# Layer 0's RMS norms taken one stream after the other, and a reordered prologue, in a two-layer fp32 backbone

## What is computed

```python
for l in range(DEPTH):                                   # DEPTH = 2
    sh1, sc1, g1, sh2, sc2, g2 = split(silu(c) @ w_mod[l] + b_mod[l])      # and mod_c from c_ctx
    h = modulate(rms_norm(x, ln1_g[l]), sh1, sc1)        # both streams
    proj = h @ w_in[l]
    att, y_conv, y_sc = attention(proj), conformer_conv(proj), short_conv(proj)
    x = x + g1 * merge_branches(gates, att, y_conv, y_sc, w_o[l])
    h2 = modulate(rms_norm(x, ln2_g[l]), sh2, sc2)
    x = x + g2 * swiglu(h2, w_ff1[l], w_ff3[l], w_ff2[l])                  # D_FF = 2816
return rms_norm(x, final_g)                              # latent stream alone
# modulate(x, shift, scale) = x * (1 + scale) + shift
# rms_norm(x, g) = x * rsqrt(mean(x * x) + eps) * g
```

## Time and profile before

| | |
|---|---|
| median of 3 runs | 1298.66 us (1297.06 to 1298.73) |
| profiled execution | 1295.26 us, span 1293.5 us |
| TensorE (PE) busy | 1230.8 us, 95% of the span |
| VectorE (DVE), ScalarE (ACT), GpSimd (POOL) busy | 876.1, 527.1, 53.5 us |
| mean granted TensorE clock | 0.984 of full speed |
| HBM read | 185.49 MB, 144 GB/s over the span |

### The profile page before, as it was taken

The page is one execution under the profiler, slowest core; times in us unless marked ns, Lnnn a source line. Parts: engine busy times, 40 slices in busy tenths (PEclk is TensorE's granted clock), DMA queues, the critical chain, the costliest instruction groups (busy, mean ns, idle before and its releaser), DMA issues.

```text
span 1293.5 us, 19441 instructions
## 1 busy us (share of the span) xinstructions
PE 1230.8 (95%) x7228; PEld 1030.4 (80%) x7228; DVE 876.1 (68%) x1344; ACT 527.1 (41%) x877; POOL 53.5 (4%) x52
## 2 busy tenths in 40 slices
PE   4999999999998979999999999799999998999997
PEld 3777776677886868888888888578789888999996
DVE  4555676768776377768765666778788766666565
ACT  4433445522423343222222223355664555644444
POOL 2000000000000300000000000300000002000002
PEclk9999999999999989999999999999999999999999
DMA  8838222124454516546565654435343574666662
GB/s 278 260 98 255 81 61 66 33 78 116 112 166 115 163 38 190 179 147 210 151 193 163 221 171 147 116 82 132 101 120 94 147 212 119 191 187 190 175 175 70
DMA packets 281601, 187.63 MB, mean 145 GB/s; under 512 B 12796, under 2 KB 270130, under 8 KB 281522
## 3 DMA queue, kind: packets, MB, share of 16 engines
q1 hardware_dynamic: 281521, 186.57, 49.5%
HBM read 185.49 MB, written 1.05 MB: 144 GB/s over the span
## 4 chain that ended last, share of the span: by engine, by line
PE 86%; DVE 6%; issue 4%; ACT 3%; DMA 1%; DVEq 0%; ACTq 0%; SPq 0%; POOL 0%; POOLq 0%
PE bank L1658 21%; PE bank L1660 21%; PE bank L1659 21%; PE scores L1910 2%; PE bank L1693 2%; PE bank L1694 2%; PE bank L1701 2%; PE bank L1893 2%; PE probsT L1919 2%; PE bank L1895 2%; PE bank L1894 2%; ACT Whi L345 2%; PE attended L1930 1%; DVE RSTD L1167 1%; DVE Wlo L356 1%
## 5 line engine op out<-in xcount | busy, mean ns | idle before, releaser
L1658 PE MATMUL bank<-Hhi,Whi 128*128 128x512 f32 (+2 forms) x1216 | 414.1, 341 | 4.7 <-DVE Wlo L356 4.7
L1659 PE MATMUL bank<-Hlo,Whi 128*128 128x512 f32 (+2 forms) x1216 | 409.7, 337 | 0.0
L1660 PE MATMUL bank<-Hhi,Wlo 128*128 128x512 f32 (+2 forms) x1216 | 409.7, 337 | 0.0
L356 DVE TENSOR_TENSOR Wlo<-Wraw,Whi 128x1024 fp32r<-128x1024 f32 (+4 forms) x328 | 320.7, 991 | 108.7 <-ACT Whi L345 107.0
L345 ACT ACTIVATE Whi<-Wraw 128x1024 fp32r<-128x1024 f32 (+4 forms) x330 | 277.7, 862 | 153.5 <-PE bank L1660 101.8
L1658 PEld LDWEIGHTS bank<-Hhi,Whi 128*128 128x128 f32 (+1 forms) x1216 | 229.9, 189 | 37.1 <-issue 7.7
L1659 PEld LDWEIGHTS bank<-Hlo,Whi 128*128 128x128 f32 (+1 forms) x1216 | 229.9, 189 | 25.7 <-issue 1.2
L1660 PEld LDWEIGHTS bank<-Hhi,Wlo 128*128 128x128 f32 (+1 forms) x1216 | 229.9, 189 | 25.3
L1658 PE MATMUL bank<-Uhi,Whi 128*128 128x512 f32 (+1 forms) x480 | 163.9, 341 | 0.6 <-DVE Ulo L1179 0.6
L1659 PE MATMUL bank<-Ulo,Whi 128*128 128x512 f32 (+1 forms) x480 | 162.3, 338 | 0.0
L1660 PE MATMUL bank<-Uhi,Wlo 128*128 128x512 f32 (+1 forms) x480 | 162.3, 338 | 0.0
(11 more groups left out here) (170 smaller groups left out, 1380.7 us busy)
## 6 DMA issues: line engine op xcount, KB each, us to landing
Wraw<-in_w_ff SPq DMA_DIRECT2D x120, 512.0 KB, 3.9
Wraw<-in_w_in SPq DMA_DIRECT2D x78, 512.0 KB, 4.0
ATT<-in_w_mod SPq DMA_DIRECT2D x58, 512.0 KB, 4.4
Wraw<-in_w_o SPq DMA_DIRECT2D x16, 512.0 KB, 3.8
ACC<-in_w_mod SPq DMA_DIRECT2D x14, 512.0 KB, 4.3
Wraw<-in_w_ff SPq DMA_DIRECT2D x16, 384.0 KB, 3.2
Wraw<-in_w_mla_o SPq DMA_DIRECT2D x8, 512.0 KB, 3.5
ATT<-in_w_mod SPq DMA_DIRECT2D x12, 256.0 KB, 5.4
```

What stands on the lines that cost most here:

```text
L356: last = eng.tensor_tensor(lo, raw, hi.bitcast(F32), ALU.subtract)
L1658: pe.matmul(dst, sh, mh, start=j == 0, stop=False)
L1659: pe.matmul(dst, sh, ml, start=False, stop=False)
L1660: last = pe.matmul(dst, sl, mh, start=False, stop=j == k - 1)
```

## The change

Four things. First, the two inner norms of layer 0 whose input comes from a product (behind w_o, and behind the FF towards layer 1) are taken stream by stream: of the last two output tiles (WHOLE = 6 on) the latent halves are computed first, then the context halves, and residual, square, sum, root, reciprocal and the normed blocks follow for each stream apart; the first tiles on the normed operand are also computed by halves. Modulation transposes that stood in or behind these places stand ahead of them, with FF_FOLDS and FF_SUMS moved by up to two tiles. Second, in the prologue x is transposed, squared and summed before ctx, by half tiles; the ten small loads are issued by ScalarE; the narrow chunk is loaded behind part 0 of the modulation weights and split behind its norm; both reciprocals stand ahead of VectorE's splits. Third, TensorE issues eight matmuls of ones by ones at the start. Fourth, at the end VectorE multiplies by the gain alone as tiles come, TensorE transposes between the last tiles, sums squares into one column per token, and the reciprocal root is applied to the transposed output by ScalarE and VectorE.

```diff
@@ constants @@
-FF_FOLDS = [4, 5, 6, 8, 9, 10, 12, 13, 14, *range(16, 27), 28, 29, 30, 32, *range(33, 65)]
-FF_SUMS = [14, 24, 34, 42, 50, 58, 66]
+FF_FOLDS = [4, 5, 6, 8, 9, 10, 12, 13, 14, *range(16, 63)]
+FF_SUMS = [14, 24, 32, 40, 48, 56, 64]
+WHOLE = DT - 2
+WARMING = 8
@@ SyncE, prologue (the ten small loads at lines 425 to 436 go) @@
-for n in range(AHEAD + 1):
+             ctx_in[0].rearrange("(t p) d -> p t d", p=P)).then_inc(x_in[1], 16)
+for n in range(AHEAD):
     project(0, n)
 ...
-sp.wait_ge(sq_done, DT)
+sp.wait_ge(sq_done, 2 * DT)
 ...
+if part == 0:
+    project(0, AHEAD)
@@ GpSimd: the last two tiles' squares are added by halves @@
+def add_halves():
+    for s in range(2):
+        look()
+        slot = at.square.n % 2
+        pool.wait_ge(sq_summed, at.added.n)
+        pool.wait_ge(sq_done, at.square.n + 1)
+        pool.tensor_tensor(SUM[:, half[s]], SUM[:, half[s]], SQ[:, slot, half[s]],
+                           ALU.add).then_inc(sq_summed, 1)
+        at.square.n += 2
+        at.added.next()
@@ ScalarE, prologue (the ten small loads stand first) @@
-for k in range(DT):
+def first_root(s):
+    act.wait_ge(sq_summed, (s + 1) * DT)
+    act.activation(ROOT[:, half[s]], (PV, S[1])[s][:, half[s]], ACT.Sqrt, bias=EPS, scale=1.0 / D).then_inc(root_done, 1)
+for i in range(2 * DT):
+    s, k = divmod(i, DT)
     t = at.tile()
     act.wait_ge(drained[t.bank], t.drained)
-    square(X[:, k, :], T, k, DT)
-at.added.n = DT
+    if i >= 2:
+        act.wait_ge(sq_summed, i - 1)
+    act.activation(SQ[:, i % 2, half[s]], X[:, k, half[s]], ACT.Square).then_inc(sq_done, 1)
+    at.square.next()
+    if i == DT + 2:
+        first_root(0)
+at.added.n = 2 * DT
 at.tile()
 look()
+first_root(1)
 look()
-act.wait_ge(sq_summed, DT)
-act.activation(ROOT[:, :], PV[:, :], ACT.Sqrt, bias=EPS, scale=1.0 / D).then_inc(root_done, 1)
 look()
 mod_row(0)
-look("rope")
@@ ScalarE, the seam @@
+look()
+for m in range(WHOLE, DT):
+    half_square(at.tile(), m, 0)
+half_root(0)
+t = at.tile()
+look()
+half_square(t, WHOLE, 1)
+for k in range(DT):
+    half_h(k, 0)
+    if k == 1:
+        half_square(at.tile(), WHOLE + 1, 1)
+    if k == 5:
+        half_root(1)
+for k in range(DT):
+    half_h(k, 1)
+at.added.n += DT
@@ VectorE, the seam and the prologue @@
+def half_h(s, between):
+    after_all()
+    for k in range(DT):
+        settle()
+        dve.scalar_tensor_tensor(Z[:, k % 2, half[s]], X[:, k, half[s]], AV[:, k, s:s + 1],
+                                 RSTD[:, half[s]], mult, mult).then_inc(z_done, 1)
+        if k:
+            half_low(k - 1, s)
+        if k in between:
+            between[k]()
+    half_low(DT - 1, s)
+roots = stat_root(0, 4) if mod else stat_root(1, 0)
+at.square.n += DT + 2
+residual(WHOLE, 0)
+look()
+residual(WHOLE + 1, 0)
+gains(l, mod, gain, 2)
+half_root(0, roots - 1)
+residual(WHOLE, 1)
+half_h(0, {1: lambda: residual(WHOLE + 1, 1), 2: look})
+half_root(1, roots)
+half_h(1, {})
 ...
-for k in range(DT):
+def first_reciprocal(s):
+    dve.wait_ge(root_done, s + 1)
+    mark(dve.reciprocal(RSTD[:, half[s]], ROOT[:, half[s]]))
+for i in range(2 * DT):
+    s, k = divmod(i, DT)
     t = full()
-    dve.tensor_copy(X[:, k, :], banks[t.bank][:, :]).then_inc(drained[t.bank], 1)
+    dve.tensor_copy(X[:, k, half[s]], banks[t.bank][:, half[0]]).then_inc(drained[t.bank], 1)
     at.square.next()
 through(t)
+first_reciprocal(0)
 t = full()
 for b, n in enumerate((ROWS, ROWS, 2 * NMOD * DT)):
     last = dve.tensor_copy(PAR[:, b, 0:n], banks[t.bank][:, b * P:b * P + n])
 last.then_inc(drained[t.bank], 1)
 through(t)
+first_reciprocal(1)
 at.split_by_slot = True
-look()
-look()
-dve.wait_ge(root_done, 1)
-mark(dve.reciprocal(RSTD[:, :], ROOT[:, :]))
-look()
-look("rope")
+for _ in range(AHEAD):
+    look()
@@ VectorE, start of layer 1, layer 0's residuals, and the end @@
-else:
-    normed_h(l, 0, 2)
-    mod_add_vector(*FF_VECTORS[-1])
-    dve.wait_ge(mod_done, at.turn)
+        if part == 0:
+            look("rope")
 ...
-    if l == 0 and j == 0:
-        dve.wait_ge(mod_done, at.turn)
-    if l == 0 and j == DT - 1:
-        mod_add_vector(0, 4, 2)
+        if l == 0:
+            dve.wait_ge(mod_done, at.turn)
     residual(j, 2)
     if j:
         look_and_fold()
-at.square.n += DT
-gains(l, 3, LN2, NS[l])
-take_root(TQ, stat_root(l, 4))
-normed_h(l, 3, NS[l])
+    if l == 0 and j == WHOLE - 1:
+        mod_add_vector(0, 4, 2)
+if l == 0:
+    seam(residual_half(2), look_and_fold, l, 3, LN2)
+else:
+    at.square.n += DT
+    gains(l, 3, LN2, NS[l])
+    take_root(TQ, stat_root(l, 4))
+    normed_h(l, 3, NS[l])
 ...
-residual(j, 5)
+through(residual(j, 5))
+finished(j)
 ...
-for k in range(DT):
-    dve.scalar_tensor_tensor(G[:, k, 0:SEQ], X[:, k, 0:SEQ], PAR[:, 3, FING + k:FING + k + 1],
-                             RSTD[:, 0:SEQ], mult, mult).then_inc(fin_z, 1)
+dve.wait_ge(root_done, stat_root(DEPTH, 0))
+dve.reciprocal(RT[:, 2:4], RT[:, 0:2]).then_inc(fin_root, 1)
+dve.wait_ge(fin_root, 1)
+for h in range(2):
+    dve.wait_ge(fin_turned, h + 1)
+    dve.tensor_scalar(X[:, 2 * h + 1, :], BY_TOKEN[1][h][:, :], RT[:, 3:4], None,
+                      mult).then_inc(out_scaled, 1)
@@ TensorE, the seam @@
+def half_product(t, slot, k, ops, s, a, b, ready):
+    oh, ol = ops
+    for j in range(a, b):
+        pe.wait_ge(op_lo, ready + j + 1)
+        w, dst = slice(j * P, (j + 1) * P), banks[t.bank][:, half[s]]
+        pe.matmul(dst, Whi[:, slot, w], oh[:, j, half[s]], start=j == 0, stop=False)
+        pe.matmul(dst, Whi[:, slot, w], ol[:, j, half[s]], start=False, stop=False)
+        last = pe.matmul(dst, Wlo[:, slot, w], oh[:, j, half[s]], start=False, stop=j == k - 1)
+    return last
+def seam_tiles(k, ops, ready):
+    slots = [chunk() for _ in range(2)]
+    squares, added = at.square.n, at.added.n
+    def half_total(t, s):
+        pe.wait_ge(sq_summed, added + DT - 1 + s)
+        pe.matmul(banks[t.bank][:, half[s]], ONES[:, :], SUM[:, half[s]], start=True, stop=False)
+        pe.wait_ge(sq_done, squares + DT + 2 * s)
+        pe.matmul(banks[t.bank][:, half[s]], ONES[:, :], SQ[:, (squares + 1) % 2, half[s]],
+                  start=False, stop=True).then_inc(tile_done, 1)
+    for slot in slots:
+        half_product(new_tile(), slot, k, ops, 0, 0, k, ready).then_inc(tile_done, 1)
+    latent, t = new_tile(), new_tile()
+    half_product(t, slots[0], k, ops, 1, 0, k // 2, ready)
+    half_total(latent, 0)
+    half_product(t, slots[0], k, ops, 1, k // 2, k, ready).then_inc(tile_done, 1)
+    half_product(new_tile(), slots[1], k, ops, 1, 0, k, ready).then_inc(tile_done, 1)
+    context = new_tile()
+    at.square.n += DT + 2
+    at.added.n += DT
+    return lambda: half_total(context, 1)
@@ TensorE, the tiles behind the seam (the last matmul of each tile in together(1, ..) signals tile_done) @@
+def staggered_tiles(ready, context_total, third_whole):
+    slots = [chunk() for _ in range(2)]
+    tiles = [new_tile() for _ in range(2)]
+    def together(s, slots, tiles, between=None):
+        r = ready + s * DT
+        for j in range(DT + 1):
+            if j < DT:
+                pe.wait_ge(op_hi, r + j + 1)
+                for t, slot in zip(tiles, slots):
+                    w, dst = slice(j * P, (j + 1) * P), banks[t.bank][:, half[s]]
+                    pe.matmul(dst, Whi[:, slot, w], Hhi[:, j, half[s]], start=j == 0, stop=False)
+                    pe.matmul(dst, Wlo[:, slot, w], Hhi[:, j, half[s]], start=False, stop=False)
+            if j:
+                pe.wait_ge(op_lo, r + j)
+                for t, slot in zip(tiles, slots):
+                    w, dst = slice((j - 1) * P, j * P), banks[t.bank][:, half[s]]
+                    last = pe.matmul(dst, Whi[:, slot, w], Hlo[:, j - 1, half[s]], start=False, stop=j == DT)
+                    if s and j == DT:
+                        last.then_inc(tile_done, 1)
+            if j == 4 and between:
+                between()
+    together(0, slots, tiles, context_total)
+    slots.append(chunk())
+    tiles.append(new_tile())
+    if third_whole:
+        half_product(tiles[2], slots[2], DT, (Hhi, Hlo), 0, 0, DT, ready)
+        together(1, slots, tiles)
+    else:
+        half_product(tiles[2], slots[2], DT, (Hhi, Hlo), 0, 0, DT - 1, ready)
+        together(1, slots[:2], tiles[:2])
+        half_product(tiles[2], slots[2], DT, (Hhi, Hlo), 0, DT - 1, DT, ready).then_inc(tile_done, 1)
@@ TensorE, prologue, start of layer 1, w_o, end @@
+for _ in range(WARMING):
+    pe.matmul(S[1][:, 0:P], ONES[:, :], ONES[:, :], start=True, stop=True)
 ...
+for i in range(2 * DT):
+    s, k = divmod(i, DT)
+    if k == 0:
+        pe.wait_ge(x_in[s], 16)
     t = new_tile()
-    for j in range(4):
-        src = G[:, 2 * j + k // 4, (k % 4) * P:(k % 4 + 1) * P]
+    for j in range(2):
+        src = G[:, 4 * s + 2 * j + k // 4, (k % 4) * P:(k % 4 + 1) * P]
```

(41 more changed lines are left out.)

197 lines of the change are left out of this document (130 added, 67 removed).

## The result

The changed kernel takes 1282.74 us (median of four executions, 1278.65 to 1283.61), the kernel before beside it 1298.10. The ratio is 0.9877, 95% interval 0.9860 to 0.9893. The profiled execution is the fastest of the four: 1278.65 us against 1295.26 before, 16.6 less, where the medians differ by 15.4. The forecast was 1281.2, or 17.5 less.

A forecast was written before the change was run, and what follows sets the result against it. The kernel was taken as bound by TensorE's matmuls, with only idle and half-clock time to win. Gains 5.6 + 3.85 + 4.8 + 3.3 = 17.5 us gave a median of 1281.2 us (profiled 1277.8), range 1277 to 1289.

The forecast's parts named there:

- Seam 1: Norm behind layer 0's w_o: taken stream by stream, 39.1 us becomes 33.5; gain 5.6 us, ends 3.0 and 6.5.
- Seam 2: Norm between layer 0's FF and layer 1: 35.75 us becomes 31.9; gain 3.85 us, ends 1.0 and 5.0.
- Rival 1: Clock falls to half in the two layer 0 norms, costing 2 to 4 us each; time 1286; chance 0.2.
- the clock read 0.50 in a seam: Sign at the two layer 0 norms: granted clock expected at 1.00 through both; 0.50 in either would make the prediction wrong.
- Prologue: Start of the kernel: TensorE's first operand matmul at 27.2 instead of 32.00; gain 4.8 us, ends 2.5 and 6.5.
- the early modulation weights: Prologue: first modulation weights issued at 10.5 instead of 15.86, landing near 20.5 and so off the path.
- the dummies: Prologue: eight dummy matmuls could delay the silu by 2 us or save up to 1.9 in transposes; taken as zero net.
- Rival 2: Prologue stays, its first operand bound by modulation weights or dummy matmuls; time 1285.7; chance 0.12.
- Tail: End of the kernel: scaling by the root moves behind the transposes; 12.65 us becomes 9.3, gain 3.3, ends 2 and 4.5.
- Rival 3: Prologue: full DMA engines hold back ScalarE's ten issues, delaying TensorE; slower than before, 1300 us and up; chance 0.04.
- rival 4: The two layer 0 norms don't overlap because a wait in TensorE's order ends late; 9 us less, 1290; chance 0.08.
- Folds: FF of layer 0: folds ending at position 62 instead of 64 fit behind the weight queue; cost 0, up to 1 us.

The follow-up runs named there:

- b1: The changed kernel with the norm behind layer 0's w_o put back as before: 1285.48 us, ratio 0.9906, 3.4 us over the changed kernel.
- b2: The changed kernel with the norm between layer 0's FF and layer 1 as before, moved modulation sum kept: 1282.65 us, ratio 0.9890.
- d1: The changed kernel with the ten small vector loads issued by SyncE again, behind the first three weight chunks: 1281.51 us, ratio 0.9877.
- a1: The changed kernel without the eight dummy matmuls at the start of TensorE's stream: 1280.6 us, ratio 0.9864.
- b3: The changed kernel with the final norm as before: 1285.98 us, ratio 0.9911, 3.9 us over the changed kernel.
- c2: The changed kernel plus dummy matmuls at waits in both layers' w_o, layer 1's norm and the FF-to-layer-1 norm: 1276.38 us, ratio 0.9835.
- c3: c2 plus dummy matmuls in the prologue (twelve and seventeen), with one of three prologue weight splits on GpSimd, two on VectorE: 1274.32 us, ratio 0.9820.
- c1: The changed kernel itself run again, beside c2 and c3: 1280.15, 1281.52 and 1282.05 us; a fourth execution of 4534 us is left out.

## Why the prediction was right, and where it was not

- **Sum.** 17.5 forecast; 16.6 in the profiled pair, 15.4 in the medians. 1.5 of the 16.6 is a clock fall near 408 that one execution had and the other had not. Without this luck the profiled pair stands at 15.1, like the medians, and what is missing from 17.5 is the prologue's 2.15. The range was sound, and wider than a wrong term of 2 us.
- **Seam 1**, 5.6: measured 5.9. The walk's parts came out: 33.2 us against 33.5, clock 1.00 throughout, TensorE waiting in three pieces (0.38, 0.95, 0.16) where I had at most 1.5 each. b1 puts it at 4.8 where the old norm gets its clock back sooner. The forecast took one execution's 5 us of half clock as fixed.
- **Seam 2**, 3.85: 3.3 in the profiled pair, and 4.8 where no fall comes (30.3 us, two transposes and the moved sum ahead, against 35.75). The walk had 31.1 to 31.9; the step was right in size, but b2 shows that 1.7 us of it was the moved modulation sum and not the staggering. Rival 1, half clock in a seam, happened in four of the ten traces with the changed seam 2 and no dummies there, and in none in seam 1, and cost 1.5 us, not 2 to 4. The rule that I weighed from the Trainium skill, "TensorE: Matmul & The Clock Gate", section "A second HAM failure mode: psum-queue depth-cycling" (frequent short pauses make the clock oscillate), is not borne out by seam 1, whose three pauses left it at 1.00 in twelve traces, and half borne out by seam 2. The prediction had called itself wrong if the clock read 0.50 in a seam. It did in seam 2 of the profiled execution (1.7 us of clock lost), so by that sign the mechanism was wrong there, and the time stood because the fall cost only 1.5 us.
- **Prologue**, 4.8: 2.65 in the pair, 2.4 over six traces. This is the term that failed, below its own lower end at the operand (2.0 against 2.5 to 6.5). By its steps: the last sum ended at 21.8, not 19.4. Of this 0.7 is the first square at 9.23 instead of 8.5: the condition vector's own transpose stood behind the eight dummies until 5.63, so that x, landed at 6.9, was transposed from 8.22 only. The other 1.7 is half clock from 9.70 to 13.18, where the steps come 1.28 apart instead of 0.65. Then the split was not shared, since it fell between GpSimd's two (1.16 for 2.49: -1.3); "from the modulation add to the first matmul 2.64" took 4.45, because the gains were locked out by GpSimd (+1.8). 27.2 + 2.4 - 1.3 + 1.8 = 30.1, measured 30.0. I copied that 2.64 from a stretch in which GpSimd had finished; moving the reciprocals ahead moved the step into GpSimd's time.
- The prologue's two other edits: the early modulation weights, which I counted as necessary, are worth nothing (d1); the dummies, taken as zero net, show no difference in time either (a1: 1280.6 without them), but in the prologue's rows they hold up the start and don't keep the transposes at full rate. Rival 2 (prologue stays) came half true, by a mechanism that it did not name.
- **Tail**, 3.3: 3.5 by rows, 3.9 by b3. **Rival 3** (ScalarE's issues): they ended at 5.66, not 4.2, before the tanh at 6.23, and delayed nothing while the dummies stood ahead of the tanh too (d1 starts its transposes at the same 8.22); without the dummies, in a1, the tanh waited for them until 5.37; **rival 4**: no trace of it. **Folds**, 0: TensorE has no new wait in the FF.

What stays open: why the clock falls in seam 2 and not in seam 1. TensorE's waits are somewhat longer in seam 2, 0.68, 0.54 and 0.95 us within 4.5 us, against 0.38, 0.95 and 0.16 in seam 1. But these waits are the same to 0.01 us in all ten traces with the changed seam 2 and no dummies, and so is TensorE's busy time beside them (1.51 of 3 us in the profiled execution from 825, 1.52 in a1 at the same place, from 826.43). The clock fell in four of the ten and stood in six. So these waits alone don't decide whether it falls. c2 and c3, with dummies there, show none, but two traces prove little where four in ten fall.

## What to carry to other kernels

Where an engine waits, ask also what the clock does behind the wait: the rows of half rate belong to the wait's price, and they differ from one execution to the next, so take them from several traces before using them as a term. When a step is moved forward in time, look up what the other engines do at its new place, above all whether GpSimd is in a long instruction while VectorE needs two operands from SBUF. And undo each part alone before crediting it: a third of a gain can come from a line that was moved on the way. When two things hold up the same step, as the dummies and ScalarE's issues do the tanh here, undoing one of them shows nothing.

## What was not expected of the hardware

- Two traces of one program can differ in whether the granted clock falls at a place. In seam 2 TensorE's waits are the same to 0.01 us in ten traces, and four of them lose 1.7 us of clock there. At the w_o of layer 1 nothing was lost in the first trace, behind waits of 2.04 and 1.13 us, and 1.7 or 3.4 us in the others, whose longest wait is 1.5 to 3.4 us. Filling such waits took 5.1 us off.
- The spread of the changed kernel, 1278.65 to 1283.61, goes in part with this. In its first four executions the mean clock is 0.992 in the shortest and 0.987 in the longest, but in the three of c1 it is 0.989 in the shortest and 0.991 in the longest. Over 99 executions of all kernels, each set against the mean of its kernel in its group, 1 us more of lost clock goes with about 0.5 us more of time (an estimate from the mean clocks of the runs).
- The granted clock reads 1.00 at the start of a1_warm0, before 15 us, while two transposes take 0.63 us each time and then 0.40: where no change is recorded yet, the durations are the witness.
- Two VectorE operations of two columns each took 2.04 us beside GpSimd's 1024-column split and 0.23 alone.
- The same transfer of 1 MB, issued at 1.89 in every trace with nothing different ahead of it on its queue, took 4.9 to 5.5 us to land in thirteen traces and 6.4 in a1.
